# Collecting the squares for the next norm behind the upper parts of half B in front of the up projections, with the sums used later

## The chip, the cores and the metric

The kernel runs on one core of one Trainium2 chip. The metric is the device time of one execution in microseconds. Smaller is better. TensorE (PE in the profile) does the matmuls, VectorE (DVE) and ScalarE (ACT) the elementwise work, GpSimd (POOL) a few sums, and SyncE's queue (SP) issues the DMAs.

## The reference, cut to what matters

Two layers, each a mixer followed by a gated ConvFFN, on 512 tokens of width 1024. Around every mixer and every FFN stands a norm before and a norm after:

```python
x = x + rms_norm(m, norm_mix_post[layer])      # m: output of the mixer
h = rms_norm(x, norm_ffn_pre[layer])
f = conv_ffn(h, w_up, conv_w, conv_b, w_down)  # gelu(g) * val, conv of width 3 on both
x = x + rms_norm(f, norm_ffn_post[layer])
```

`rms_norm(x, g)` is `x * rsqrt(mean(x*x) + 1e-6) * g`, the mean over the 1024 columns of one token. So the norm in front of the up projection needs, for each token, the sum of the squares of the new x.

## The kernel before, in words

Activations stand with their columns on the partitions: x is 8 tiles of 128 columns by 512 tokens. Every operand of a matmul is split into an upper part (hi) and the rest (lo), and each product is three matmuls: hi by hi, hi by lo, lo by hi (L1559 to L1561). A unit is 256 columns of a weight matrix. Its weights are loaded by a DMA (w_raw), ScalarE makes w_hi (`split_hi`, L674) and VectorE w_lo (`split_lo`, L1050). TensorE waits for w_lo of a unit before it begins it.

The order on each engine is written out by hand; semaphores tie the engines together. Between two stages stands a `boundary`. There are three: bi 0 between the first mixer and the up projection of layer 0, bi 1 between layer 0 and the second mixer, and bi 2 between the second mixer and the up projection of layer 1. A boundary works on two halves of the tokens, A and B (256 tokens each). Per half and tile i:

- VectorE: `normed` (L1330) and `add` (L1336) make the new x, `lo` (L1340) makes hx_lo from x and hx_hi. `lo(i)` stands in front of `normed(i+2)` and `add(i+2)`. In half B of bi 0 and 2 a `split_lo` stands between `add(7)` and `lo(6)`, and another behind `lo(7)`.
- ScalarE: `hi` (L872) makes hx_hi. In half B, `square` (L682) follows each `hi` and squares that tile for all 512 tokens into one of two buffers. Behind tile 5 stands a `split_hi`.
- GpSimd: `pre_norm` (L625, L628) adds the eight tiles of squares up into `sumsq`, 7 additions one after the other. `square(i)` for i from 2 on waits for the addition that frees its buffer: square 2 and 3 for the first addition, square 4 for the second, and so on.
- TensorE: `first_units` works the first two units of the up projection (called u and u+1 here), first on half A, then on half B with a wait for hx_ready, raised by `lo`, in front of every tile. Then comes unit u+2, as 48 matmuls in an order of two column blocks by eight tiles: hook (b, k) stands in front of the three matmuls of block b and tile k. `mean_square` (L1619) is 8 small matmuls on `sumsq` and `spread` (L1651) the matmul that lays the factor over all partitions.

The unnormalised h is multiplied first, and its result is scaled by the factor of each token. The factor comes so: `mean_square` on TensorE, `root` (L686) on ScalarE, `inverse_rms` (L1057, L1060) on VectorE, `spread` on TensorE, copy to rbc (L1074) on VectorE. Only then can VectorE's `ffn_up` take the first unit out of PSUM (`ug`, `uv`, L1377 and L1378). `ffn_up` then goes through the units one by one, VectorE and ScalarE in turn: ug, uv, the centre taps on ScalarE (L914, L918), four taps (L1386), the GeLU, the product (L1393), g_hi (L926), g_lo (L1395). In the same order stand the splits of the weights of later units: `ffn_up` of u splits unit u+4, those of u+1 and u+2 split nothing, that of u+3 splits unit u+5, and so on. PSUM holds three units at a time: unit u+3 needs that u has been taken out.

At bi 1 the stage behind the boundary is the projection to q, k, v, and its third unit has hooks of its own.

Of the kernel before, what the change touches and what calls it, by code (L numbers as in the profile page):

```python
# [24 lines left out]
DT = D // P  # L25
# [44 lines left out]
def group_of(u):  # L70

    shift = 0
    for layer in range(2):
        if u >= U_DOWN[layer] + N_DOWN:
            shift += G_SHIFT
        elif u >= U_DOWN[layer]:
            return U_DOWN[layer] - shift + (u - U_DOWN[layer]) // len(DOWN_K)
    return u - shift
# [23 lines left out]
def pre_sums(p):  # L102

    return (DT - 1) * p


def a_halves(bi):

    return (0, 3, 4)[bi]
# [20 lines left out]
def slot(u):  # L130

    if u in OWN_SLOT:
        return RING + OWN_SLOT.index(u)
    return (u - sum(u > x for x in OWN_SLOT)) % RING
# [7 lines left out]
def loaded_at(u):  # L142

    return 16 * sum(dmas_of(v) for v in range(2, u + 1) if slot(v) == slot(u))


def build(nc, io, out):
# [22 lines left out]
    def place(name, shape, dt):  # L170
        t = at(name, shape, dt, where[0])
        where[0] += size(shape, dt)
        return t
# [7 lines left out]
    x = place("x", [P, DT, T], F32)  # L181
# [123 lines left out]
    def bank(b, n=1):  # L305
        return ps[:, T * b:T * (b + n)]
# [18 lines left out]
    def tokens_of(h):  # L325

        return slice(HALF * h, HALF * h + HALF)
# [90 lines left out]
    def gain(which, layer, i):  # L418

        c = 16 * which + 8 * layer + i  # L420
        return vec[:, c:c + 1]
# [246 lines left out]
    def _(act):  # L668
        def split_hi(u, k=UK, i=None, per=RING, cnt=0):

            s = slot(u)
            at_ = loaded_at(u)
            act.wait_ge(w_loaded[s], at_ if i is None else i * cnt + at_)
            act.activation(w_hi[s][:, 0:k], w_raw[s][:, 0:k], ACT.Copy).then_inc(w_hi_done, 1)  # L674

        def square(p, i, src):

            if i >= 2:
                act.wait_ge(sum_done, pre_sums(p) + max(1, i - 2))
            elif p:  # L680
                act.wait_ge(pms_mm, 2 * p)
            act.activation(sq[i % 2][:], src, ACT.Square).then_inc(sq_done, 1)  # L682

        def root(p):
            act.wait_ge(ms_mm, p + 1)
            act.activation(std[:], bank(7)[:, 0:TT], ACT.Sqrt, scale=1.0 / D, bias=eps).then_inc(std_done, 1)  # L686
# [13 lines left out]
        def post_root(bi, h):  # L700
            act.wait_ge(pms_mm, 2 * bi + h + 1)
            act.activation(std[:, 2 * h:2 * h + 2], bank(7)[:, 2 * h:2 * h + 2], ACT.Sqrt, scale=1.0 / D, bias=eps).then_inc(pstd_done, 1)
# [148 lines left out]
        def half_out(bi, h, j, u):  # L851

            i = 3 if bi == 1 else 1 + j
            half_square(bi, h, j, u)
            act.activation(m[:, 2 * i:2 * i + 2, tokens_of(h)], halves(out_half_bank(u, h)),
                           ACT.Copy).then_inc(group_evac if h else ahalf_evac, 1)

        def raw(i):

            u = ROPE_UNITS[i]  # L860
            act.wait_ge(unit_done, u + 1)
            if i >= 2:
                act.wait_ge(rope_done, 2 * i)
            for b in range(2):
                act.activation(halves(rp[i % 2][b][:]), out_tile(u, group_banks(group_of(u)), b), ACT.Copy,
                               scale=SCALE if i else 1.0).then_inc(rope_raw, 1)

        def boundary(bi, which, layer, last, splits):

            def hi(h, i):  # L870
                act.wait_ge(x_new, 2 * DT * bi + DT * h + i + 1)
                act.activation(hx_hi[:, i, tokens_of(h)], x[:, i, tokens_of(h)], ACT.Identity,  # L872
                               scale=gain(which, layer, i)).then_inc(hx_hi_done, 1)

            act.preload_act_table_set("sqrt_and_others")
            for j, v in enumerate(last):
                half_out(bi, 0, j, v)
            post_root(bi, 0)
            if bi != 1:
                half_out(bi, 1, 0, last[0])  # L880
            for i in range(DT):
                hi(0, i)
                if i == (4 if bi == 1 else 3):
                    split_hi(splits[0])
                if i == 5 and bi != 1:
                    half_out(bi, 1, 1, last[1])
            half_out(bi, 1, len(last) - 1, last[-1])
            split_hi(splits[1])
            post_root(bi, 1)
            for i in range(DT):  # L890
                hi(1, i)
                square(bi + 1, i, x[:, i, :])
                if i == (3 if bi == 1 else 5):
                    split_hi(splits[2])
            if bi == 1:
                raw(0)
            root(bi + 1)
# [658 lines left out]
    def _(pe):  # L1556
# [6 lines left out]
        def unit_ready(u, i=None):  # L1563

            pe.wait_ge(w_lo_done, u + 1 if i is None else i * RING + (u + 1))

        def banks_free(g, i=None):

            if i is not None:
                pe.wait_ge(group_evac, i * RING + evacuated(g - 3))  # L1570
            elif g >= 3:
                q = g - G_QKV
                if 3 <= q <= 7:
                    pe.wait_ge(rope_cos, {3: 2, 4: 4, 5: 6, 6: 8, 7: 10}[q])
                elif q == 8:
                    pe.wait_ge(ex_done, SW_STEPS)
                else:
                    pe.wait_ge(group_evac, evacuated(g - 3))
# [5 lines left out]
        def columns(u, ks, src, b0, k_first=0, k_last=UK - 1, koff=0, signal_first=False, hooks=None):  # L1584

            for b in range(2):
                for k in ks:
                    if hooks and (b, k) in hooks:
                        hooks[b, k]()
                    last = three(bank(b0 + b), *weights(u, k, b), src[0][:, k + koff, :], src[1][:, k + koff, :],  # L1590
                                 k + koff == k_first, k + koff == k_last)
                if signal_first and b == 0:
                    last.then_inc(m_first, 1)
            return last
# [14 lines left out]
        hx = (hx_hi, hx_lo)  # L1609
# [3 lines left out]
        def mean_square(p):  # L1613

            if p:
                pe.wait_ge(pstd_done, 2 * p)
            pe.wait_ge(sum_done, pre_sums(p + 1))
            for t in range(TT):
                last = pe.matmul(bank(7)[:, t:t + 1], sumsq[:, P * t:P * t + P], ones[:, 0:1], start=t == 0, stop=t == TT - 1)  # L1619
            last.then_inc(ms_mm, 1)  # L1620
# [27 lines left out]
        def spread(n):  # L1648

            pe.wait_ge(diag_done, n + 1)  # L1650
            pe.matmul(bank(6 if n else 4), ones, diag[:].rearrange("p t c -> p (t c)"), start=True, stop=True).then_inc(bc_mm, 1)  # L1651
# [17 lines left out]
        def unit(u, src, i=None, hooks=None):  # L1669
            g = group_of(u)  # L1670
            banks_free(g, i)
            unit_ready(u, i)
            columns(u, range(UK), src, group_banks(g), signal_first=src is y, hooks=hooks).then_inc(unit_done, 1)
# [254 lines left out]
        def first_units(bi, u):  # L1928

            a_copied, evac = a_halves(bi) + (1 if bi == 1 else 3), evacuated(group_of(u) - 1)  # L1930
            pe.wait_ge(ahalf_evac, a_copied)
            for j in range(2):
                unit_ready(u + j)
                for k in range(UK):
                    if j == 0 and k == 3:
                        post_mean_square(bi, 1)
                    if j == 0 and k == 6:
                        post_spread(bi, 1)
                    pe.wait_ge(hx_ready, DT + 2 * DT * bi + k + 1)
                    first_half(u + j, 0, k)  # L1940
            pe.wait_ge(group_evac, evac)
            for k in range(UK):
                pe.wait_ge(hx_ready, 2 * DT + 2 * DT * bi + k + 1)
                for j in range(2):
                    last = first_half(u + j, 1, k)
                    if k == UK - 1:
                        last.then_inc(unit_done, 1)
            if bi == 1:
                banks_free(group_of(u + 2))
                unit_ready(u + 2)  # L1950
                tokens(u + 2, group_banks(group_of(u + 2)),
                       {(0, 2): lambda: mean_square(2), (1, 4): lambda: spread(2)}).then_inc(unit_done, 1)
            else:
                unit(u + 2, hx, hooks={(0, 1): lambda: mean_square(bi + 1), (0, 6): lambda: spread(bi + 1)})

        def ffn(layer, bi):
            u0 = U_UP[layer]
# [237 lines left out]
```

## Time and profile before

| | |
|---|---|
| median of 3 runs | 1126.22 us (1125.81 to 1127.9) |
| the profiled execution, its own time | 1126.66 us |
| its span, first to last instruction | 1123.8 us |
| TensorE busy | 1106.1 us, 98% |
| VectorE busy | 681.4 us, 61% |
| ScalarE busy | 500.7 us, 45% |
| GpSimd busy | 68.5 us, 6% |

The span is divided between engines that run at the same time. Busy shares are means over the whole kernel; what one edit is worth is read at its own place, in the timelines. In a timeline a row has the start, the duration, the engine and line, the operation, and in brackets how long the engine idled in front of it and on whom. TensorE's weight loads (PEld) run beside its matmuls.

### The profile page before, as it was taken

To read this page: it belongs to the slowest core of one execution; us is meant where nothing else is said; L and a number is where in the kernel's file an instruction comes from. 1 tells how busy PE (TensorE), PEld (TensorE's weight loads), DVE (VectorE), ACT (ScalarE), POOL (GpSimd) and SP (SyncE) were. 2 spreads that over 40 slices of the span, in tenths; PEclk is the share of its full clock that TensorE was granted. 3 is DMA by queue.
4 is the path that set the end of the run, shared out by engine and by line. 5 is a ranking of instruction groups with operands and counts; after the bars stand their busy time and mean duration, and the time that the engine had idled before them with its cause. 6 is when DMAs were issued, how large, how long until landed. Compare 5 with 4: busy or idle time off the path is not lost.

```text
span 1123.8 us, 15368 instructions
## 1 busy us (share of the span) xinstructions
PE 1106.1 (98%) x6036; PEld 936.4 (83%) x6036; DVE 681.4 (61%) x899; ACT 500.7 (45%) x699; POOL 68.5 (6%) x56
## 2 busy tenths in 40 slices
PE   8999999999999999999999999999999999999997
PEld 7878778998888888888899877898788888888886
DVE  5675477587776767732248677378877676662313
ACT  5556766544443443422225356564434344342311
POOL 3000000240000000000013000023000000000000
PEclk9999999999999999999999999999999999999999
DMA  7311111413242333332222625131424233231322
GB/s 224 113 53 61 53 60 47 132 49 112 76 112 77 110 97 90 103 101 80 101 66 77 183 69 157 50 102 38 113 75 112 82 105 103 84 113 57 113 94 75
DMA packets 141991, 104.41 MB, mean 93 GB/s; under 512 B 4658, under 2 KB 133362, under 8 KB 141938
## 3 DMA queue, kind: packets, MB, share of 16 engines
q1 hardware_dynamic: 141906, 103.66, 30.8%
q8 instruction: 38, 0.62, 0.2%
q14 instruction: 15, 0.12, 0.0%
q10 hardware_dynamic: 32, 0.01, 0.0%
HBM read 98.02 MB, written 2.10 MB: 89 GB/s over the span
## 4 chain that ended last, share of the span: by engine, by line
PE 82%; DVE 9%; issue 3%; ACT 3%; DMA 2%; SPq 1%; DVEq 0%; ACTq 0%
PE ps L1559 25%; PE ps L1561 25%; PE ps L1560 25%; PE ps L1780 2%; SPq L542 1%; DVE hx_lo L1340 1%; DVE w_lo L1050 1%; DVE ps L1330 1%; DVE x L1336 1%; PE ps L1764 1%; PE ps L1793 1%; DVE cv L1386 1%; DVE cg L1386 1%; PE ps L1635 1%; ACT prob L1005 1%
## 5 line engine op out<-in xcount | busy, mean ns | idle before, releaser
L1559 PE MATMUL ps<-hx_hi,w_hi 128*128 128x512 f32 (+1 forms) x944 | 360.8, 382 | 4.4 <-DVE w_lo L1082 1.9
L1561 PE MATMUL ps<-hx_hi,w_lo 128*128 128x512 f32 (+1 forms) x944 | 354.0, 375 | 0.0
L1560 PE MATMUL ps<-hx_lo,w_hi 128*128 128x512 f32 (+1 forms) x944 | 353.9, 375 | 0.0
L1050 DVE TENSOR_TENSOR w_lo<-w_raw,w_hi 128x2048 fp32r<-128x2048 f32 (+2 forms) x87 | 194.9, 2241 | 150.3 <-ACT w_hi L674 150.2
L674 ACT ACTIVATE w_hi<-w_raw 128x2048 fp32r<-128x2048 f32 (+2 forms) x87 | 162.6, 1870 | 141.8 <-DMA w_raw<-in_ffn_w_down 113.7
L1559 PEld LDWEIGHTS ps<-hx_hi,w_hi 128*128 128x128 f32 x944 | 177.7, 188 | 39.8 <-issue 4.6
L1561 PEld LDWEIGHTS ps<-hx_hi,w_lo 128*128 128x128 f32 x944 | 177.7, 188 | 32.4
L1560 PEld LDWEIGHTS ps<-hx_lo,w_hi 128*128 128x128 f32 x944 | 177.8, 188 | 31.9 <-issue 1.7
L914 ACT ACTIVATE cg<-ug,vec 128x512 f32<-128x512 f32 x44 | 35.9, 816 | 141.5 <-DVE ug L1377 141.5
L1386 DVE SCALAR_TENSOR_TENSOR cg<-ug,vec,cg 128x511 f32<-128x511 f32 x88 | 65.8, 748 | 21.9 <-ACT cg L914 21.9
L926 ACT ACTIVATE g_hi<-cv 128x512 f32 (+1 forms) x44 | 27.8, 632 | 112.1 <-DVE cv L1393 112.1
L1559 PE MATMUL ps<-g_hi,w_hi 128*128 128x512 f32 (+1 forms) x220 | 76.5, 348 | 0.0
L1560 PE MATMUL ps<-g_lo,w_hi 128*128 128x512 f32 (+1 forms) x220 | 76.2, 347 | 0.0
L1561 PE MATMUL ps<-g_hi,w_lo 128*128 128x512 f32 (+1 forms) x220 | 76.2, 347 | 0.0
L1559 PE MATMUL ps<-w_hi,g_hi 128*128 128x512 f32 x176 | 68.8, 391 | 0.0
L1561 PE MATMUL ps<-w_hi,g_lo 128*128 128x512 f32 x176 | 68.5, 389 | 0.0
L1560 PE MATMUL ps<-w_lo,g_hi 128*128 128x512 f32 x176 | 68.5, 389 | 0.0
L1377 DVE TENSOR_TENSOR ug<-ps,rbc 128x512 f32<-128x512 f32 x44 | 30.4, 690 | 61.2 <-PE ps L1561 61.1
L1386 DVE SCALAR_TENSOR_TENSOR cv<-uv,vec,cv 128x511 f32<-128x511 f32 x88 | 65.8, 748 | 0.0
L1395 DVE TENSOR_TENSOR g_lo<-cv,g_hi 128x512 f32 (+1 forms) x44 | 30.5, 693 | 37.8 <-ACT g_hi L926 37.8
L1560 PEld LDWEIGHTS ps<-g_lo,w_hi 128*128 128x128 f32 x220 | 41.7, 189 | 5.3
L1559 PEld LDWEIGHTS ps<-g_hi,w_hi 128*128 128x128 f32 x220 | 41.7, 189 | 5.2
(235 smaller groups left out, 1650.3 us busy)
## 6 DMA issues: line engine op xcount, KB each, us to landing
w_raw<-in_ffn_w_up SPq DMA_DIRECT2D x84, 512.0 KB, 4.5
w_raw<-in_ffn_w_down SPq DMA_DIRECT2D x18, 1024.0 KB, 5.0
w_raw<-in_even_w_in SPq DMA_DIRECT2D x8, 1024.0 KB, 5.0
w_raw<-in_odd_w_qkv SPq DMA_DIRECT2D x6, 1024.0 KB, 5.1
w_raw<-in_even_w_out SPq DMA_DIRECT2D x4, 1024.0 KB, 5.0
w_raw<-in_ffn_w_down SPq DMA_DIRECT2D x4, 768.0 KB, 4.3
w_raw<-in_odd_w_o SPq DMA_DIRECT2D x3, 1024.0 KB, 5.2
rsw<-rp SPq DMA_DIRECT2D x40, 64.0 KB, 2.0
```

The lines of the kernel that those rows point to most:

```text
L542: sp_.dma_start(rsw[i % 2][b][32 * a:32 * a + 32, :], rp[i % 2][b][32 * c:32 * c + 32, :]).then_inc(rope_sw[i % 2][b], 16)
L674: act.activation(w_hi[s][:, 0:k], w_raw[s][:, 0:k], ACT.Copy).then_inc(w_hi_done, 1)
L914: act.activation(cg[:], ug[:], ACT.Identity, scale=col(ffn_vec(layer, 2, j)), bias=col(ffn_vec(layer, 3, j))).then_inc(center, 1)
L926: act.activation(tile_(g_hi, j), cv[:], ACT.Copy).then_inc(g_hi_done, 1)
L1050: dve.tensor_tensor(w_lo[s][:, 0:k], w_raw[s][:, 0:k], w_hi[s][:, 0:k], ALU.subtract).then_inc(w_lo_done, 1)
L1377: dve.tensor_tensor(halves(ug[:]), out_tile(u, b0, 0), halves(rbc[:]), ALU.mult).then_inc(scaled, 1)
L1386: dve.scalar_tensor_tensor(out=dst[:, s:], in0=src[:, 0:T - s], scalar=col(ffn_vec(layer, 2 - s, j + FT * b)), in1=dst[:, s:], op0=ALU.mul ...
L1395: dve.tensor_tensor(tile_(g_lo, j), cv[:], tile_(g_hi, j), ALU.subtract).then_inc(g_ready, 1)
L1559: pe.matmul(dst, s_hi, r_hi, start=first, stop=False)
L1560: pe.matmul(dst, s_hi, r_lo, start=False, stop=False)
L1561: return pe.matmul(dst, s_lo, r_hi, start=False, stop=last)
L1780: last = pe.matmul(ps[:, c0:c0 + n], (tri_r if jj == j else ones_r)[:], part[:, OFF[jj]:OFF[jj] + n], start=False, stop=(jj == TT - 1 and ...
```

## The change

It touches the boundaries bi 0 and bi 2. On ScalarE the eight `square` instructions, one behind each `hi` of half B, now stand together behind the last `hi` (and so also behind the `split_hi`). On TensorE the hooks in unit u+2 move: `mean_square` from (0, 1) to (0, 6), `spread` from (0, 6) to (1, 2). No instruction is added or left out. At bi 1 all stays.

```diff
             post_root(bi, 1)
             for i in range(DT):
                 hi(1, i)
-                square(bi + 1, i, x[:, i, :])
+                if bi == 1:
+                    square(bi + 1, i, x[:, i, :])
                 if i == (3 if bi == 1 else 5):
                     split_hi(splits[2])
+            if bi != 1:
+                for i in range(DT):
+                    square(bi + 1, i, x[:, i, :])
             if bi == 1:
                 raw(0)
             root(bi + 1)
@@ TensorE, first_units
-                unit(u + 2, hx, hooks={(0, 1): lambda: mean_square(bi + 1), (0, 6): lambda: spread(bi + 1)})
+                unit(u + 2, hx, hooks={(0, 6): lambda: mean_square(bi + 1), (1, 2): lambda: spread(bi + 1)})
```

## Rows read from the trace of the kernel before

**Rows 1.** The page: busy time of TensorE, share of span, instructions.
```profile
PE 1106.1 (98%) x6036; PEld 936.4 (83%) x6036; DVE 681.4 (61%) x899; ACT 500.7 (45%) x699; POOL 68.5 (6%) x56
```
**Rows 2.** Waits of TensorE, whole span: who for whom, us in total, times, longest.
```profile
PE ps L1559 <- DVE w_lo L1050: 1.7, 3, 0.8
PE ps L1559 <- DVE hx_lo L1340: 1.6, 3, 0.6
```
**Rows 3.** Timeline of GpSimd, half B of the first boundary.
```profile
235.60 1.29 POOL L625 TENSOR_TENSOR sumsq<-sq,sq 128x512 f32<-128x512 f32 x1 [10.32 <-ACT sq L682]
237.63 1.29 POOL L628 TENSOR_TENSOR sumsq<-sumsq,sq 128x512 f32<-128x512 f32 x1 [0.74 <-ACT sq L682]
245.46 4.49 POOL L628 TENSOR_TENSOR sumsq<-sumsq,sq 128x512 f32<-128x512 f32 x2 [1.42 <-ACT sq L682]
```
**Rows 4.** Timeline of VectorE, the same stretch, a few of its rows.
```profile
234.38 0.48 DVE L1340 SCALAR_TENSOR_TENSOR hx_lo<-x,vec,hx_hi 128x256 fp32r<-128x256 f32 x1
235.63 1.54 DVE L1340 SCALAR_TENSOR_TENSOR hx_lo<-x,vec,hx_hi 128x256 fp32r<-128x256 f32 x1
...
245.09 2.28 DVE L1050 TENSOR_TENSOR w_lo<-w_raw,w_hi 128x2048 fp32r<-128x2048 f32 x1
247.30 2.94 DVE L1340 SCALAR_TENSOR_TENSOR hx_lo<-x,vec,hx_hi 128x256 fp32r<-128x256 f32 x2
250.16 2.28 DVE L1050 TENSOR_TENSOR w_lo<-w_raw,w_hi 128x2048 fp32r<-128x2048 f32 x1
```
**Rows 5.** Timeline of ScalarE, the same stretch, a few of its rows.
```profile
233.52 0.51 ACT L872 ACTIVATE hx_hi<-x,vec 128x256 fp32r<-128x256 f32 x1 [3.32 <-DVE x L1336]
233.93 0.61 ACT L682 ACTIVATE sq<-x 128x512 f32<-128x512 f32 x1
234.49 0.51 ACT L872 ACTIVATE hx_hi<-x,vec 128x256 fp32r<-128x256 f32 x1
...
242.57 1.90 ACT L674 ACTIVATE w_hi<-w_raw 128x2048 fp32r<-128x2048 f32 x1
```
**Rows 6.** Timeline of TensorE, end of half B and beginning of unit u+2.
```profile
247.95 0.28 PE L1561 MATMUL ps<-hx_hi,w_lo 128*128 128x256 f32 x1
248.86 0.38 PE L1559 MATMUL ps<-hx_hi,w_hi_x 128*128 128x256 f32 x1 [0.64 <-DVE hx_lo L1340]
...
250.40 0.29 PE L1559 MATMUL ps<-hx_hi,w_hi_x 128*128 128x256 f32 x1
251.81 0.40 PE L1559 MATMUL ps<-hx_hi,w_hi 128*128 128x512 f32 x1
252.51 0.95 PE L1619 MATMUL ps<-const,sumsq 128*128 128x1 f32 x8
253.32 0.48 PE L1559 MATMUL ps<-hx_hi,w_hi 128*128 128x512 f32 x1
256.82 1.02 PE L1651 MATMUL ps<-diag,const 128*128 128x512 f32 x2
```
**Rows 7.** Timeline of VectorE, the factor copied and the first unit taken out.
```profile
257.87 0.69 DVE L1074 COPY rbc<-ps 128x512 f32<-128x512 f32 x1 [2.99 <-PE ps L1651]
259.21 0.68 DVE L1378 TENSOR_TENSOR uv<-ps,rbc 128x512 f32<-128x512 f32 x1
```
**Rows 8.** Waits of VectorE from 258 to 287 us.
```profile
DVE g_lo L1395 <- ACT g_hi L926: 2.1, 3, 0.7
DVE cg L1386 <- ACT cg L914: 1.5, 4, 0.7
```
**Rows 9.** Timeline of VectorE and TensorE where unit u+5 begins.
```profile
284.60 2.29 DVE L1050 TENSOR_TENSOR w_lo<-w_raw,w_hi 128x2048 fp32r<-128x2048 f32 x1
286.94 0.50 PE L1559 MATMUL ps<-hx_hi,w_hi 128*128 128x512 f32 x1 [0.50 <-DVE w_lo L1050]
```
**Rows 10.** Timeline, second of the two boundaries: two rows of TensorE.
```profile
770.96 0.38 PE L1559 MATMUL ps<-hx_hi,w_hi_x 128*128 128x256 f32 x1 [0.64 <-DVE hx_lo L1340]
809.31 0.50 PE L1559 MATMUL ps<-hx_hi,w_hi 128*128 128x512 f32 x1 [0.78 <-DVE w_lo L1050]
```

## The prediction, made before the changed kernel was run

> **What bounds the kernel now.** I read the page first: TensorE is busy for 1106.1 us, 98% of the span, all others for 61% or less [rows 1]. So an edit on another engine moves the time only by what TensorE waits for. Second, TensorE's waits: six short ones concern us, three for hx_lo (1.6 us in all) and three for w_lo of a later unit (1.7 us) [rows 2]. Third, the timelines of the four engines side by side at the two boundaries that the edit touches. At the first, TensorE waits once in half B, for `lo(6)`: the last matmul of tile 5 starts at 247.95, the next at 248.86 [rows 6]. It waits a second time 38 us later, for the w_lo of unit u+5: that split ends at 286.89 and TensorE restarts at 286.94 [rows 9]. The second boundary repeats both, 522.1 and 522.4 us later [rows 10]. Where these two waits come from decides the case.
>
> The first comes from GpSimd. A `lo` alone lasts 0.48 us, but 1.54 us beside the addition that runs from 235.60 to 236.89, and the last two together 2.94 us [rows 3, 4]. It works the other way as well: the sixth addition was issued at 245.46, into the `split_lo` of 245.09 to 247.37, and the pair of additions took 4.49 us instead of 2 x 1.29 [rows 3, 4]. So one waits while the other runs, and the split was not slowed: it had come first.
>
> The second comes from the factor rbc. From its copy at 257.87 on, VectorE and ScalarE hand the units of `ffn_up` to each other; VectorE's idle time from 258 to 287 us is all for ScalarE's cg and g_hi, 0.3 to 0.7 us at a time, none for TensorE or a DMA [rows 8]. The split for u+5 stands in the fourth `ffn_up`, so it ends 29.0 us after the copy begins (286.89 - 257.87), wherever that falls [rows 7, 9]. **TensorE starts u+5 when rbc says so**, not when it has finished u+4.
>
> **Removed: squares and additions from half B.** Undisturbed, a tile takes VectorE 1.25 us (`lo(0)` 234.38, `lo(1)` 235.63 [rows 4]). `lo(5)` then starts at 234.38 + 5 x 1.25 = 240.6 and the split behind `add(7)` at 241.9 instead of 245.09: 3.2 us won. It ends at 244.2. `lo(6)` follows at 244.1 and `lo(7)` before 246.1 even if the first of them is held up by an addition to 1.47 us. TensorE needs them at 248.1 and 249.5. The wait in half B goes: 248.86 - 248.07 = 0.8 us, and 0.13 us of a slow restart (that tile took 1.54 us, the next 1.41 [rows 6]). **Worth 0.9 us** per boundary; unit u+2 starts at 250.9 instead of 251.81.
>
> **Moved: the eight squares.** `hi(1)` starts at 234.49 and each next 1.25 us later, `hi(5)` at 239.5. The `split_hi` follows 0.42 us later and lasts 1.90 us, to 241.8; `hi(6)` and `hi(7)` take 0.42 each, square 0 starts at 242.6, square 1 ends at 243.7 [rows 5]. The squares themselves cost nothing: ScalarE's next work is `root`. The split is passed by the squares and keeps its place behind `hi(5)`; its input is in either way, since it began at 242.57 without a wait [rows 5]. No DMA is moved.
>
> **Moved: the seven additions.** Addition 1 asks at 243.8, in the middle of the split that runs to 244.2. It runs to 245.45. Square 2 waits for it, and addition 2 asks 0.74 us after it (as at 237.63 [rows 3]), at 246.2. But by then VectorE, ahead of time, has begun the last `split_lo` at 245.9; before it began at 250.16, when all additions were over [rows 4]. It holds addition 2 until 248.2, which ends at 249.45. Five more at 1.33 us (1.29 and a little between) end at **256.1**, against 249.95 before. Bounds: 254.1, if the split does not hold addition 2 (246.2 + 1.29 + 5 x 1.33); 257.2, if VectorE goes from split to `lo` to split and lets no addition in before 247.2 (that + 1.29 + 2.03 + 5 x 1.33).
>
> The Trainium skill has the rule for this (SBUF — State Buffer, section "Who interferes with whom"): a VectorE instruction with two SBUF inputs and a GpSimd instruction that reads SBUF exclude each other for a whole instruction, and the order of issue decides who waits. The trace agrees where both kinds meet, 1.54 us against 0.48. The page speaks for the edit in half B and against it behind half B, where the lock turns round on the additions.
>
> **Moved: the two hooks.** A matmul of 512 columns takes 0.23 us in the stream (15 from 253.32 to 256.82 [rows 6]). TensorE reaches (0, 6) at 250.9 + 18 x 0.23 = 255.0 and waits there for the sums until 256.1 or 256.2: **1.1 us of a new wait**. Nothing but the rest of u+2 is queued behind it. `mean_square` costs 0.8 us as before (252.51 to 253.32 [rows 6]), the 12 matmuls to (1, 2) 2.8 us: `spread` at 256.2 + 0.8 + 2.8 = 259.8, against 256.82. `root` and `inverse_rms` fit in between: they have 3.6 us, and before VectorE had its part done 2.99 us ahead of 257.87, so 2.4 us after 252.51 [rows 6, 7]. So rbc comes **2.9 us later**, at 260.8 instead of 257.87.
>
> Unit u+3 does not feel it: the banks of u come free with uv, 259.89 before [rows 7], 262.8 now, and u+3 starts near 264.6 (250.9 + 48 x 0.23 + 1.1, and some 0.8 for each hook). Unit u+4 starts 11 us after that, and its weights are split in the first of the four `ffn_up` that share the 29 us.
>
> **The sum.** Up to u+5 TensorE wins 0.9 and loses 1.1 us, some 0.2 us late. At u+5 it waits for a split that now ends 2.9 us later: 289.8 instead of 286.9. The start of u+5 moves by the full 2.9 us, and the 0.9 us won in half B is swallowed by that wait. Behind it VectorE catches up with TensorE, and nothing gives the time back: loads go out when units end, so they move too. Twice 2.9 is 5.8 us. On the profiled execution that is 1126.66 + 5.8 = 1132.5 us; the median of the runs lies 0.4 us below that execution, so **1132.0 us**.
>
> **The rivals.**
>
> Sums in time, hooks alone. If the additions are through by 255.0, `mean_square` starts at its new place without a wait and `spread` at 255.0 + 0.8 + 2.8 = 258.6, 1.8 us later than before. Twice 1.8 gives 1129.8 us. For it: the bound of 254.1. Against it: the split in rows 4 that held an addition. This is the lower end of slower.
>
> Additions shut out longer. If VectorE keeps its turn through `lo(6)`, `lo(7)` and the last split, the sums end at 257.2, `spread` starts at 257.3 + 0.8 + 2.8 = 260.9 and rbc moves 4.1 us, in all 1134.4 us. Against it: at 247.37 a waiting addition got in between a split and a `lo` that was ready [rows 3, 4].
>
> The wait at u+5 has slack. If the fourth `ffn_up` could close up, only TensorE's own balance would count, 1.1 - 0.9 us per boundary: 1126.6 us, no change. Against it: VectorE idles in that stretch only for ScalarE, and ScalarE for VectorE [rows 8].
>
> **Faster than before**: the freed VectorE wins the 0.9 us in half B and the chain to u+5 gets no later, so the wait there (0.5 and 0.8 us [rows 9, 10]) could go too. That gives 2 x 0.9 + 1.3 = 3.1 us, 1123.1 us. It decides as soon as rbc comes no later than before; for that TensorE would have to reach `spread` at (1, 2) by 256.8, and its own 30 matmuls and `mean_square` from 250.9 already end at 258.6. I see no way.
>
> **How the numbers follow.** Forecast (1131 to 1133): 0.60. Hooks alone: 0.18. Shut out longer: 0.10. Slack, no change: 0.09. Faster: 0.03. The first three are slower by over 0.2%, which is about what a measurement of this kernel can tell from no change (2.3 us): 0.88, of which 0.01 of the hooks' case, 1129.8, is lost to the noise: 0.87. Same 0.10, faster 0.03. The range takes in the hooks alone and the additions shut out: 1128.9 to 1134.6 us.
>
> **What the profile of the changed kernel would show.** Half B without a wait for hx_lo, every `lo` but one or two at 0.48 us. TensorE waits about 1 us at L1619's matmuls for sumsq, twice. An addition of over 3 us beside the last split. rbc about 2.9 us later against the start of half B. TensorE waiting 3 us for w_lo at u+5 instead of 0.5 to 0.8. Wrong would be: no longer wait at u+5 (then the chain had slack), or additions and splits side by side without lengthening (then the sum falls to the hooks' 3.6 us).

## The result

The changed kernel takes **1138.3 us** (median of 6 runs, 1134.5 to 1139.4) against 1126.1 us beside it: ratio 1.0098, 95% interval 1.0088 to 1.0108. It is slower by 12.2 us. The direction was as forecast, the time lies above the range (1128.9 to 1134.6), and the loss is twice the 5.8 us of the sum.

The profiled execution took 1136.6 us, its span is 1134.6 us, 10.8 us more than before. The busy time of TensorE, which answers to [rows 1], rose although it has the same 6036 matmuls:

```profile
PE 1110.6 (98%) x6036; PEld 939.5 (83%) x6036; DVE 673.0 (59%) x899; ACT 501.6 (44%) x699; POOL 69.5 (6%) x56
```

Second, TensorE's waits over the whole span, in the form of [rows 2] (the lines of TensorE and VectorE stand 4 further down now):

```profile
PE ps L1563 <- DVE w_lo L1054: 6.9, 3, 3.5
PE ps L1623 <- POOL sumsq L628: 2.9, 2, 1.5
...
PE ps L1563 <- DVE hx_lo L1344: 0.4, 1, 0.4
```

The waits for hx_lo at the two changed boundaries are gone (0.4 us is left of 1.6, at another boundary). A wait for the sums is new, 1.5 us twice. The wait for w_lo has grown from 1.7 to 6.9 us. Net that is 6.9 us more waiting for 10.8 us of time; the rest must lie in the busy time.

Third, the timelines of the first boundary, as in [rows 3, 4, 6, 7, 9]. Everything in this execution lies 0.25 us earlier than before until half B begins. GpSimd, then VectorE, then TensorE:

```profile
243.50 1.59 POOL L625 TENSOR_TENSOR sumsq<-sq,sq 128x512 f32<-128x512 f32 x1 [18.33 <-ACT sq L682]
245.83 10.42 POOL L628 TENSOR_TENSOR sumsq<-sumsq,sq 128x512 f32<-128x512 f32 x6 [0.74 <-ACT sq L682]
```
```profile
241.65 2.28 DVE L1054 TENSOR_TENSOR w_lo<-w_raw,w_hi 128x2048 fp32r<-128x2048 f32 x1
243.85 1.91 DVE L1344 SCALAR_TENSOR_TENSOR hx_lo<-x,vec,hx_hi 128x256 fp32r<-128x256 f32 x2
245.69 2.28 DVE L1054 TENSOR_TENSOR w_lo<-w_raw,w_hi 128x2048 fp32r<-128x2048 f32 x1
...
261.19 0.69 DVE L1078 COPY rbc<-ps 128x512 f32<-128x512 f32 x1 [2.35 <-PE ps L1655]
...
287.91 2.28 DVE L1054 TENSOR_TENSOR w_lo<-w_raw,w_hi 128x2048 fp32r<-128x2048 f32 x1
```
```profile
250.69 0.40 PE L1563 MATMUL ps<-hx_hi,w_hi 128*128 128x512 f32 x1
...
256.40 1.02 PE L1623 MATMUL ps<-const,sumsq 128*128 128x1 f32 x8 [1.44 <-POOL sumsq L628]
260.13 1.02 PE L1655 MATMUL ps<-diag,const 128*128 128x512 f32 x2
290.25 0.50 PE L1563 MATMUL ps<-hx_hi,w_hi 128*128 128x512 f32 x1 [3.21 <-DVE w_lo L1054]
```

The reader finds each step of the forecast: the split in half B at 241.65, the first addition held up, the second issued at 245.83 into the last split, six additions in 10.42 us, TensorE waiting for them, rbc copied at 261.19 instead of 257.87, and unit u+5 started at 290.25 instead of 286.94, 29.06 us after the copy began (before: 29.07). The second boundary shows more:

```profile
817.36 0.80 PE L1563 MATMUL ps<-hx_hi,w_hi 128*128 128x512 f32 x1 [3.52 <-DVE w_lo L1054]
817.95 0.63 PE L1564 MATMUL ps<-hx_lo,w_hi 128*128 128x512 f32 x1
818.38 0.63 PE L1565 MATMUL ps<-hx_hi,w_lo 128*128 128x512 f32 x1
```

Behind this wait the matmuls are 0.43 us apart instead of 0.23. The view by stretches says why. A row has the stretch and its length, the busy time of TensorE, of its weight loads, of VectorE, ScalarE and GpSimd with their counts, then the mean granted clock, the DMA share and GB/s:

```profile
286.00:290.00 4.00, 1.04 (x5) 0.54 (x3) 4.00 (x4) 2.08 (x2) 0.00 (x0) 1.00 0.32 91
290.00:294.00 4.00, 3.75 (x10) 3.02 (x11) 2.69 (x5) 1.42 (x3) 0.00 (x0) 0.61 0.62 171
812.00:816.00 4.00, 1.84 (x9) 1.19 (x7) 3.63 (x5) 2.99 (x3) 0.00 (x0) 1.00 0.13 37
816.00:820.00 4.00, 2.64 (x6) 2.16 (x7) 3.05 (x4) 0.63 (x1) 0.00 (x0) 0.56 0.81 227
...
820.00:830.00 10.00, 10.00 (x38) 8.07 (x37) 7.02 (x9) 4.48 (x5) 0.00 (x0) 0.83 0.01 2
```

**The granted clock went to its lower level, 1.2 GHz, behind both waits at u+5**, for some 3.4 us at the first boundary and 6.8 us at the second. That is read from the means: at half speed, 0.56 over 4 us and 0.83 over 10 us are 3.5 and 3.4 us; 0.61 over 4 us is 3.1 us, and the next 4 us have the remainder at 0.97. In the kernel before the clock is at 1.00 in the same places:

```profile
290.00:294.00 4.00, 4.00 (x19) 3.30 (x19) 3.45 (x6) 3.75 (x4) 0.00 (x0) 1.00 0.38 105
812.00:818.00 6.00, 6.00 (x28) 4.99 (x27) 5.46 (x7) 3.85 (x4) 0.00 (x0) 1.00 0.29 74
```

By the records of the granted clock the low stretch at the second boundary began at 816.51, inside the wait, so 0.85 us of its 6.83 us cost nothing.

So the 10.8 us divide. At the first boundary half B begins 0.24 us early and u+5 starts 3.31 us late, so the factor costs 3.55 us there. The end of unit u+6, seen by the next ug on VectorE (314.07 against 309.16), is 4.91 us late: 1.6 us came with the clock. The second half B begins only 4.48 us late (its first `normed` at 759.11 against 754.63), so 0.43 us came back in between; where was not followed up. There u+5 starts 8.05 us late, 3.57 us of it from the factor, and u+6 ends 10.82 us late (842.37 against 831.55): 2.8 us with the clock. The late factor costs 7.1 us, the clock 4.4 us, the two small shifts give 0.7 us back, and behind u+6 nothing more is lost.

### The profile page after: what moved, and what is told of

It reads as the page before. It is cut to its first block, busy times and chain, and to the rows that moved or that the text cites. A ratio compares the mean times of both kernels' runs of the same rounds, so it can differ in the third digit from the quotient of the medians.

```text
span 1134.6 us, 15368 instructions
## 1 busy us (share of the span) xinstructions
PE 1110.6 (98%) x6036; PEld 939.5 (83%) x6036; DVE 673.0 (59%) x899; ACT 501.6 (44%) x699; POOL 69.5 (6%) x56
## 4 chain that ended last, share of the span: by engine, by line
PE 83%; DVE 7%; ACT 3%; issue 2%; POOL 2%; DMA 1%; SPq 1%; DVEq 0%; POOLq 0%; ACTq 0%
PE ps L1563 25%; PE ps L1565 25%; PE ps L1564 25%; PE ps L1784 2%; POOL sumsq L628 2%; DVE w_lo L1054 1%; PE ps L1768 1%; PE ps L1797 1%; DVE ps L1334 1%; DVE cv L1390 1%; DVE cg L1390 1%; DVE x L1340 1%; PE ps L1639 1%; ACT prob L1009 1%; SPq L542 1%
```

## The experiments

Two theories stood at the start. Mine: the factor comes late, u+5 hangs on it, and the clock falls because TensorE has stood still. The rivals: one half of the edit is harmless and the other does all; or the clock falls by itself.

**e1, the squares alone.** The hooks stay at (0, 1) and (0, 6).

```diff
-hooks={(0, 6): lambda: mean_square(bi + 1), (1, 2): lambda: spread(bi + 1)}
+hooks={(0, 1): lambda: mean_square(bi + 1), (0, 6): lambda: spread(bi + 1)}
```

> The squares stand behind half B as in the changed kernel; the hooks stay where they were, at (0, 1) and (0, 6). Theory of the late factor: the sums end when they end, near 256.0 us, so TensorE waits some 4.6 us at mean_square instead of 1.4, and spread follows 15 matmuls later instead of 12, which makes the factor another 0.6 us later. At u+5 only about 0.7 to 1 us of waiting is left, and u+5 starts some 4 us later than in the kernel before, about 8 us in all without the clock. Rival, the moved hooks are what costs: then this kernel is near the kernel before, within 2 us. For the clock: the changed kernel shows the lower level of the granted clock behind its waits of 3.2 and 3.5 us; if the length of a wait is what brings it, this kernel shows it behind mean_square and not behind u+5.

Measured: 1141.0 us, ratio 1.0127 (1.0108 to 1.0146). From TensorE's timeline, and by stretches:

```profile
257.26 1.84 PE L1623 MATMUL ps<-const,sumsq 128*128 128x1 f32 x8 [4.79 <-POOL sumsq L628]
294.39 0.50 PE L1563 MATMUL ps<-hx_hi,w_hi 128*128 128x512 f32 x1 [0.49 <-DVE w_lo L1054]
```
```profile
252.00:256.00 4.00, 0.47 (x3) 0.04 (x1) 0.00 (x0) 1.40 (x3) 3.57 (x4) 1.00 0.68 201
256.00:260.00 4.00, 2.74 (x11) 2.57 (x12) 0.53 (x3) 0.26 (x1) 1.12 (x1) 0.50 0.25 62
290.00:294.00 4.00, 3.90 (x18) 2.89 (x16) 4.00 (x5) 2.23 (x2) 0.00 (x0) 1.00 0.00 0
```

The last number but two of a row is the clock. The wait moved to `mean_square` (4.8 us, twice), 0.5 and 0.8 us are left at u+5, and the low clock moved with it: 0.50 behind the long wait, 1.00 where the changed kernel had 0.61. The clock follows the wait, not the place. The loss is 14.8 us where I had 8 without the clock, and the low clock costs more here than its own stretch: the matmuls between `mean_square` and `spread` ran in it, 7.0 us from one to the other instead of 4.3 (264.27 - 257.26, 256.82 - 252.51), so the factor came later still, and u+5 starts 7.45 us late where I had 4. So moving the hooks back does not save the time, it costs 2.7 us more: with the squares where they are, the sums are late, and the later hooks only let TensorE do more of u+2 first.

**e2, the hooks alone.** The kernel before with only the second hunk of the diff.

> Only the hooks are moved, to (0, 6) and (1, 2); the squares stay one behind each upper part. Theory of the late factor: no wait at mean_square, the wait for hx_lo in half B stays (0.6 us), spread comes 12 matmuls later, 2.7 us, and the wait for w_lo at u+5 grows from 0.5 to about 3.2 us (0.8 to 3.5 at the second boundary): 5.4 us slower, and up to 5 us more if the clock falls behind the waits as it does in the changed kernel. Rival, the sums behind the lock are what costs: then nothing is lost here, and the kernel is within 1 us of the kernel before.

Measured: 1135.0 us, ratio 1.0078 (1.0056 to 1.0100).

```profile
256.61 0.95 PE L1619 MATMUL ps<-const,sumsq 128*128 128x1 f32 x8
260.27 1.02 PE L1651 MATMUL ps<-diag,const 128*128 128x512 f32 x2
290.38 0.80 PE L1559 MATMUL ps<-hx_hi,w_hi 128*128 128x512 f32 x1 [3.21 <-DVE w_lo L1050]
```

No wait for sums, and yet 3.2 and 3.5 us at u+5, as many as in the changed kernel. Each half of the edit alone is slower than the kernel before: whichever makes rbc late pays at u+5. The two do not add up (14.8 and 8.7 us against 12.2): the factor needs both the sums and TensorE's arrival at its hooks, and the later of the two decides.

**e3, the changed kernel with u+5 freed of the factor.** The splits of u+5, u+6 and u+7 stand one `ffn_up` earlier. Three rounds of the loop are written out for it; the same work in the same order of units.

```diff
-    def split_at(layer, u):
-        return {0: u + 4, 1: None, 2: None}.get(u - U_UP[layer], u + 2)
+    def split_at(layer, u, i):
+        if i is not None:
+            return u + 2
+        return {0: u + 4, 1: None, 2: u + 3, 3: u + 3, 4: u + 3, 5: None}.get(u - U_UP[layer], u + 2)
@@ ffn of ScalarE; VectorE's has the same with dve.Fori
-            for j in range(3):
+            for j in range(6):
                 ffn_up(layer, j, U_UP[layer] + j)
-            with act.Fori(0, 5) as i:
+            with act.Fori(1, 5) as i:
```

> The changed kernel, but units u+5, u+6 and u+7 are split one ffn_up earlier (in those of u+2, u+3 and u+4, none in that of u+5), so that the start of u+5 no longer hangs on the factor. Theory of the late factor: no wait at u+5 at all and no fall of the clock; what is left is the 1.4 us at mean_square against the 0.9 us won in half B and the 0.5 to 0.8 us that the kernel before waits at u+5: between 1125 and 1127 us. Rival, the time goes in some other place (the waits at mean_square, or the clock falls by itself): then 1133 us or more remain.

Measured: 1128.2 us (10 runs, 1126.2 to 1131.9), ratio 1.0019 (1.0009 to 1.0030). The wait at u+5 is gone, and with it 10 of the 12 us. The time is 1.2 us above my upper figure. I had expected no fall of the clock, but behind the 1.45 us wait for the sums it fell at the first boundary (second row), not at the second (third row), where the wait is as long. From the start of u+2 to that of u+6 TensorE needs 48.64 us at the first and 47.09 us at the second, so the fall cost 1.6 us. The profiled execution, with this one fall, took 1126.9 us, inside my figures. What made the median 1.3 us longer is not shown: most of the runs have the same mean granted clock as the profiled one, 0.997, only the slowest has 0.993.

```profile
257.04 1.02 PE L1625 MATMUL ps<-const,sumsq 128*128 128x1 f32 x8 [1.45 <-POOL sumsq L630]
```
```profile
256.00:260.00 4.00, 2.96 (x13) 2.54 (x14) 1.05 (x5) 0.26 (x1) 0.90 (x1) 0.77 0.15 36
780.00:784.00 4.00, 3.67 (x20) 3.24 (x21) 1.05 (x5) 0.26 (x1) 0.19 (x1) 1.00 0.00 0
```

**e4, the last split out of the additions' way.** The changed kernel, with VectorE's last split of the boundary behind `inverse_rms`.

```diff
-            if bi != 1:
-                split_lo(splits[2])
             inverse_rms(bi + 1)
+            if bi != 1:
+                split_lo(splits[2])
             spread(bi + 1)
```

> The changed kernel, but VectorE's last split of weights in the boundary stands behind inverse_rms instead of in front of it, so that no VectorE instruction with two operands in SBUF runs beside additions 2 to 7. Theory of the port: additions 2 to 7 take 1.3 us each (7.8 us together instead of 10.4), the wait at mean_square falls from 1.4 us to nothing, the factor comes about 1 us earlier, and the wait at u+5 is about 2.3 us instead of 3.2: about 2 us faster than the changed kernel, and more if the clock does not fall. Rival, the additions are slow for another reason: they stay at 10.4 us and nothing changes.

Measured: 1133.1 us (1131.9 to 1133.7), 5.2 us faster than the changed kernel's median; ratio to before 1.0058 (1.0041 to 1.0074).

```profile
247.34 8.46 POOL L628 TENSOR_TENSOR sumsq<-sumsq,sq 128x512 f32<-128x512 f32 x6 [0.74 <-ACT sq L682]
```
```profile
256.32 0.95 PE L1623 MATMUL ps<-const,sumsq 128*128 128x1 f32 x8
290.09 0.80 PE L1563 MATMUL ps<-hx_hi,w_hi 128*128 128x512 f32 x1 [3.21 <-DVE w_lo L1054]
```

The additions lose 2.0 us and TensorE no longer waits for them: the split was what held them. They take 8.46 us, not 7.8: one stands every 1.43 us, not every 1.33. And the wait at u+5 did not shrink to 2.3 us as I wrote. The factor comes earlier, but TensorE, without its wait of 1.4 us, comes to u+5 earlier by as much. In this one profile u+5 starts some 1.7 us earlier against its own half B, at each boundary; that makes 3.4 of the 5.2 us. The clock was low for 3.4 us behind the second wait, not for 6.8, which saves another 1.2 us (u+5 takes 12.61 us there instead of 13.82). Some 0.6 us between the medians are not assigned.

**e5, the kernel before with the early splits** (the diff of e3 alone).

> The kernel before, with units u+5, u+6 and u+7 split one ffn_up earlier and nothing else. Theory of the late factor: the start of u+5 hung on the factor in the kernel before too, so its waits of 0.5 and 0.8 us go (the gaps there are 0.65 and 0.9 us) and the kernel is 1.5 us faster, 1124.7 us. Rival, that wait is bound by something else (the load, the banks): nothing changes.

Measured: 1123.9 us (11 runs, 1123.1 to 1126.1) against 1126.2 us, ratio 0.9982 (0.9973 to 0.9991). The wait at u+5 hung on the factor in the kernel before too. The gain is 2.3 us where I had 1.5; in the profiles 0.8 and 1.1 us of it lie at the two boundaries (u+2 to u+6 takes 45.35 us at both, before 46.17 and 46.46), the rest is not assigned. This run moves the split alone; that the tie is to the factor, and in what size, e7 shows.

**e6, the changed kernel with early splits and later hooks**, at (1, 0) and (1, 3).

```diff
-hooks={(0, 6): lambda: mean_square(bi + 1), (1, 2): lambda: spread(bi + 1)}
+hooks={(1, 0): lambda: mean_square(bi + 1), (1, 3): lambda: spread(bi + 1)}
```

> The changed kernel with the early splits and with the hooks at (1, 0) and (1, 3), so that the sums, which end near 256.1 us, are there when TensorE comes to mean_square. Theory: half B keeps its 0.9 us, no wait at mean_square, none at u+5, no fall of the clock at either: 3.3 us faster than the kernel before, 1123 us, and its runs lie as close together as those of the kernel before. Rival, the moved squares do harm that is not seen yet (ScalarE or the port): then it is not faster than the kernel before with early splits, 1124.7 us.

Measured: **1123.1 us** (8 runs, 1122.5 to 1124.3), ratio 0.9973 (0.9963 to 0.9984): 3.1 us faster than the kernel before, 15.2 us faster than the changed one. TensorE's longest waits over the whole span now lie outside these two stages:

```profile
PE ps L1565 <- DVE w_lo L1088: 1.5, 2, 1.0
PE ps L1565 <- DVE y_lo L1529: 1.5, 2, 1.3
```

The moved squares do no harm by themselves. Whether they help cannot be told from e5: the medians differ by 0.8 us and the intervals overlap, though the wait for hx_lo (0.66 and 0.64 us in e5) is not there in e6. The later hooks are not free either: the sums end at 257.07, TensorE waits some 0.3 us for them, `mean_square` starts at 257.22, and u+2 to u+6 takes 45.73 and 45.74 us, 0.4 us more than in e5. So about 0.5 of the 0.9 us of half B would be left per boundary, which fits the 0.8 us between the medians but is not clear of their noise.

**e7, only the spread later**, from (0, 6) to (1, 0) in the kernel before, 6 matmuls.

> The kernel before with only spread moved, from (0, 6) to (1, 0): 6 matmuls, 1.36 us. Theory of the late factor: each us that the factor comes later is a us of waiting at u+5, so the waits there grow from 0.5 and 0.8 to 1.9 and 2.2 us and the kernel is 2.7 us slower, 1128.8 us, without the clock. The waits lie between 1.4 us, behind which the clock fell at one of two places in the changed kernel with early splits, and 3.2 us, behind which it fell every time: if it falls here too, up to 1.7 us more for each place. Rival: a later factor costs nothing by itself, and the time stays at 1126.2 us.

Measured: 1130.5 us (5 runs, 1129.6 to 1132.0), ratio 1.0039 (1.0025 to 1.0052), 4.3 us slower.

```profile
258.20 1.02 PE L1651 MATMUL ps<-diag,const 128*128 128x512 f32 x2
288.32 0.50 PE L1559 MATMUL ps<-hx_hi,w_hi 128*128 128x512 f32 x1 [1.85 <-DVE w_lo L1050]
812.50 0.50 PE L1559 MATMUL ps<-hx_hi,w_hi 128*128 128x512 f32 x1 [2.15 <-DVE w_lo L1050]
```
```profile
288.00:292.00 4.00, 3.68 (x16) 3.08 (x17) 2.76 (x5) 1.35 (x2) 0.00 (x0) 1.00 0.92 255
812.00:818.00 6.00, 5.50 (x17) 4.36 (x18) 4.50 (x8) 3.16 (x4) 0.00 (x0) 0.72 0.59 167
```

`spread` comes 1.38 us later and u+5 starts 1.38 us later (286.94, now 288.32): one for one. The clock stayed up behind 1.85 us and fell behind 2.15 us. Twice 1.38 us and one fall at 1.6 us are 4.4 us; 4.3 us were measured.

## Why the prediction was wrong

By its own steps:

- **Half B.** Right: u+2 starts at 250.69, which is 250.9 less the 0.25 us by which this execution is ahead.
- **The additions.** Right in mechanism: the last split holds the second one, and e4 shows it by taking the split away. The interval was short, 1.33 us where the runs show 1.43: it was put at one addition "and a little between", and [rows 3] have no longer row of additions than a pair whose first was held. The sums ended near 256.25 and not at 255.85 (both in this profile's time).
- **The wait at mean_square.** 1.1 us forecast, 1.44 and 1.47 measured, mostly from that interval.
- **The factor.** 2.9 us later forecast. Measured against the start of half B: 3.6 us at both boundaries.
- **u+5 moves with the factor, one for one.** Right, and the step on which the sign rested: 29.06 us from copy to start, e7 in size, e3 and e5 by taking the tie away. My rival with slack in that chain is refuted.
- **The sum.** Here the prediction failed. "Twice 2.9 is 5.8 us" is wrong in two ways. The smaller one is the size of the factor's term, 7.1 us measured where it says 5.8; with that alone the time would be 1126.2 + 7.1 = 1133.3 us, still in the range. The larger one is a term that the sum doesn't have: it priced each us of waiting as one us, with TensorE at full clock behind it. But behind a wait of over 3 us TensorE ran at half its clock for 3.4 or 6.8 us, which cost 1.6 and 2.8 us in the profile. In other runs it cost more: the mean granted clock is 0.993 in the three slowest (1138.8 to 1139.4 us), 0.995 in the profiled one. 0.002 of the span is 4.5 us more at the low level, 2.3 us of time, and 1136.6 + 2.3 = 1138.9. The profiled execution is closed by these terms (7.1 + 4.4 - 0.7 = 10.8 us). For the median, 1.7 us above it, the clock has the right size; where it fell in those runs no trace shows.
- **A count.** The prediction speaks of six waits that concern it. Two of them lie elsewhere (0.43 us for w_lo at 204 us, 0.35 us for hx_lo at 619 us). The sum uses the right four.

The trace of before has no wait of TensorE longer than 1.4 us, and the clock is at its full level behind all of them, so it showed neither the fall nor its price. A wait that the sum makes four to seven times as long as those in the trace (0.5 and 0.8 us to over 3 us) has left what the trace can price at face value, and the range should have been left open upwards for it.

The rival that ended faster was right in where the gain lay. Its condition was that rbc comes no later. The gain is also there when u+5 no longer asks for rbc: e6 does that and takes 3.1 us, the figure of that rival, by another way than its condition. That the figure is the same is luck: e5 alone takes 2.3 us, where the rival put 1.3 us at u+5, and e6 adds 0.8 us to that, where it put 1.8 us in half B.

## What to carry to other kernels

A wait removed in one place is worth nothing if a later one hangs on a chain that starts later: look for the next place where the bound engine waits, and for the event from which its end is counted. When a serial chain runs behind the bound engine, take what that engine needs out of the chain (here a split of weights, one step ahead) before touching its head. And price a wait of TensorE that grows beyond those in the trace at more than its length: here 3.2 to 3.5 us of waiting cost 1.6 to 2.8 us on top.

## What the runs showed of the hardware

The granted clock behind waits of TensorE, in the profiled executions of all these kernels: behind 0.5 to 1.0 us it stayed at its full level, every time, and so it did behind the wait of 1.3 us for y_lo that every kernel has near 710 us. Behind 1.44 to 1.48 us at `mean_square` it fell at one of four places (in e3); behind 1.85 us it stayed and behind 2.15 us it fell (e7); behind 3.2 to 3.5 us it fell at all six places (the changed kernel, e2, e4); behind 4.8 us at both (e1). Length alone does not decide: a wait of 1.80 us near 10 us in e4 brought no fall.

It was low for 3.41 or 6.83 us each time. The six stretches of 3.41 us began between 0.15 us before the end of the wait and 1.3 us behind it, the four of 6.83 us began 0.8 to 1.3 us before its end (changed kernel, e1 twice, e2). A stretch of 3.41 us costs 1.5 to 1.6 us, one of 6.83 us behind u+5's wait 2.6 to 2.8 us. The Trainium skill (TensorE: Matmul & The Clock Gate, section "Part 1: The HAM clock gate") says that a gate in front of the array sets the clock by how busy it has been of late; that the low stretch moved to `mean_square` with the wait, in e1, agrees. The times of the kernels with such waits mostly lie further apart, 4.9 us in the changed kernel and 5.6 us in e3 against 1.8 us in e6 and 3.0 us in e5, but four runs of e4 lie within 1.8 us too.

Between an instruction of VectorE with two operands in SBUF and an addition of GpSimd the order of issue decided who waited, in both directions in one kernel: additions made a `lo` 1.06 us longer before, the last split made an addition 2.0 us longer after (10.42 us for six, 8.46 us in e4). Moving work of one of the two does not remove the meeting, it picks a new partner.
